# Six 256-column matmuls per weight tile, summed in one PSUM bank per group, in place of two of 512 columns and two of 256 over two banks

## What is computed

```python
def hybrid_layer(x, mem, ...):
    h = rmsnorm(x, g_mix)
    proj = h @ w_in
    fq, fk, fv, ff, lx, lg, mq, gate_logits = jnp.split(proj, cuts, axis=-1)
    ...
    y_fox = forgetting_attention(q, k, v, log_f)
    xr = causal_depthwise_conv(lx, w_lru_conv, b_lru_conv)
    y_lru = rg_lru(xr, w_rg_a, b_rg_a, w_rg_x, b_rg_x, lru_lambda) * jax.nn.gelu(lg)
    mk, mv = jnp.split(rmsnorm(mem, g_mem) @ w_mem_kv, 2, axis=-1)
    ...
    y_mem = memory_attention(qm, km, vm)
    branches = jnp.stack([y_fox, y_lru, y_mem], axis=2)
    y_d = jnp.einsum('bsnc,ncd->bsnd', branches, w_branch)
    gates = jax.nn.sigmoid(gate_logits.reshape(b, s, N_BRANCH, D_MODEL) + b_gate)
    merged = jnp.sum(gates * y_d, axis=2)
    x = x + merged @ w_out
    up = causal_depthwise_conv(rmsnorm(x, g_ffn) @ w_ffn_up, w_ffn_conv, b_ffn_conv)
    u_act, u_val = jnp.split(up, 2, axis=-1)
    return x + (jax.nn.gelu(u_act) * u_val) @ w_ffn_down
```

## Time and profile before

| | us |
|---|---|
| median of 3 runs | 1662.53 |
| lowest and highest run | 1662.39, 1663.37 |
| span of the profiled execution | 1661.6 |
| TensorE matmuls busy in the span | 1641.6 |
| TensorE weight loads busy | 1426.6 |
| VectorE busy | 1117.1 |
| ScalarE busy | 895.9 |

### The profile page before, as it was taken

The page is one execution under the profiler, slowest core; times in us unless marked ns, Lnnn a source line. Parts: engine busy times, 40 slices in busy tenths (PEclk is TensorE's granted clock), DMA queues, the critical chain, the costliest instruction groups (busy, mean ns, idle before and its releaser), DMA issues.

```text
span 1661.6 us, 27207 instructions
## 1 busy us (share of the span) xinstructions
PE 1641.6 (99%) x9356; PEld 1426.6 (86%) x9356; DVE 1117.1 (67%) x1324; ACT 895.9 (54%) x1145; POOL 54.9 (3%) x57
## 2 busy tenths in 40 slices
PE   7999999999999999999999999999999999999998
PEld 6888888888888888888888888888888888888887
DVE  6977677678847566575666777777777777544443
ACT  6766567466644544545455555555555555434332
POOL 0010112000000000000001000000000000000000
PEclk9999999999999999999999999999999999999999
DMA  8544456553555555555565555555555655655653
GB/s 301 195 151 162 150 172 200 188 167 126 177 185 185 191 187 190 189 189 190 177 192 189 176 190 200 189 179 189 192 178 185 202 189 186 201 197 196 202 195 102
DMA packets 85833, 307.37 MB, mean 185 GB/s; under 512 B 9944, under 2 KB 11232, under 8 KB 85664
## 3 DMA queue, kind: packets, MB, share of 16 engines
q1 hardware_dynamic: 84672, 302.89, 55.0%
q0 software_dynamic: 1120, 3.94, 0.8%
HBM read 304.69 MB, written 2.11 MB: 185 GB/s over the span
## 4 chain that ended last, share of the span: by engine, by line
PE 94%; DVE 2%; issue 2%; ACT 1%; DMA 1%; SPq 0%; POOL 0%; ACTq 0%; DVEq 0%; POOLq 0%
PE psG L315 91%; PE psM L315 2%; DVE fox_rstd L910 1%; DVE W L885 1%; DMA mem_raw<-memT 0%; ACT W L554 0%; DMA lru_rg<-w_rg 0%; PE psM L406 0%; ACT fox_rstd L593 0%; DVE fox_S L938 0%; DVE stat L941 0%; DVE fox_q_n L926 0%; ACT L554 0%; ACT fox_S L583 0%; ACT fox_S L605 0%
## 5 line engine op out<-in xcount | busy, mean ns | idle before, releaser
L315 PE MATMUL psG<-X,W 128*128 128x512 f32 (+1 forms) x5632 | 993.2, 338 | 0.0
L315 PEld LDWEIGHTS psG<-X,W 128*128 128x128 f32 x5632 | 860.4, 188 | 128.1 <-issue 2.4
L885 DVE TENSOR_TENSOR W<-raw,W 128x1024 fp32r<-128x1024 f32 x567 | 687.8, 1227 | 314.9 <-ACT W L554 312.2
L554 ACT ACTIVATE W<-raw 128x1024 fp32r<-128x1024 f32 x567 | 591.2, 1054 | 318.7 <-PE psG L315 314.6
L315 PE MATMUL psG<-hidden,W 128*128 128x512 f32 (+1 forms) x1408 | 245.4, 337 | 0.0
L315 PEld LDWEIGHTS psG<-hidden,W 128*128 128x128 f32 x1408 | 214.0, 188 | 31.3
L562 ACT ACTIVATE low<-psG 128x512 f32<-128x512 f32 x140 | 83.8, 598 | 224.6 <-PE psG L315 224.6
L315 PE MATMUL psG<-Y,W 128*128 x768 | 134.4, 337 | 0.0
L315 PEld LDWEIGHTS psG<-Y,W 128*128 128x128 f32 x768 | 117.0, 188 | 17.1
L1300 DVE SCALAR_TENSOR_TENSOR up_c<-up_pad,par_sb,up_c 128x256 f32<-128x256 f32 x176 | 77.5, 482 | 42.3 <-ACT up_c L829 36.3
L315 PE MATMUL psG<-merged,W 128*128 128x512 f32 (+1 forms) x512 | 89.3, 337 | 0.0
(11 more groups left out here) (185 smaller groups left out, 672.5 us busy)
## 6 DMA issues: line engine op xcount, KB each, us to landing
raw<-w_units SPq DMA_DIRECT2D x567, 512.0 KB, 3.4
xs<-xT SPq DMA_DIRECT2D x4, 512.0 KB, 9.8
outT<-xs POOLq DMA_DIRECT2D x7, 256.0 KB, 3.6
mem_raw<-memT SPq DMA_DIRECT2D x3, 512.0 KB, 9.0
lru_rg<-w_rg POOLq DMA_DIRECT2D x8, 128.0 KB, 4.3
c_all<-c_rows POOLq DMA_DIRECT2D x1, 1024.0 KB, 8.8
mem_raw<-memT SPq DMA_DIRECT2D x4, 128.0 KB, 2.5
raw<-w_units SPq DMA_DIRECT2D x2, 256.0 KB, 3.2
```

The lines of the kernel that those rows point to most:

```text
L315: return nc.tensor.matmul(*a, skip_group_check=True, **kw)
L554: nc.scalar.activation(W[:, s, :, 0], raw[:, s], ACT.Copy).then_inc(hi_done, 1)
L885: V.tensor_tensor(W[:, s, :, 1], raw[:, s], f32(W[:, s, :, 0]), ALU.subtract).then_inc(lo_done, 1)
```

## The change

Each weight tile is now worked on by six matmuls of 256 columns. They are ordered by stationary part: for the high weights, half `t` = 0 against high activations, then again `t` = 0 against low activations, then both for `t` = 1; then the low weights against the high activations for both halves (in the `rows_major` phases with weights and activations exchanged). All three products of a half go to the same 256 columns, and both halves lie in one bank, so a group has one bank, `psG` has two, and the sum is complete in PSUM. `start` is set on the first matmul of the bank alone.

So nothing is left to add: `low`, `copy_low`, `add_low` and `yd` are gone, and the reader takes the bank directly. Which engine empties which group is in a table (`EMPTIED_BY`): ACT copies the groups of mv, lru, v, qk and the query of mkq (`empty`) and takes `Tanh` of the gates from the bank; DVE scales the key of mkq, multiplies the branches, adds the residual in out and down, and scales up from the bank. In place of `evac_done` there are two counters, `emptied_act` and `emptied_dve`. Where ACT now writes a destination that a DVE step of the iteration before still reads, ACT waits for that step (`normed` in qk and mkq, `gelu` and `lru_taps` in lru).

```diff
+EMPTIED_BY = {"mv": "aa", "mkq": "da", "lru": "aa", "v": "aa", "qk": "aa", "gate": "aa", "branch": "dd",
+              "out": "dd", "up": "dd", "down": "dddd"}
...
-        psG = ctx.enter_context(nc.psum_tensor("psG", [P, 4, 512], F32))
+        psG = ctx.enter_context(nc.psum_tensor("psG", [P, 2, 512], F32))
...
+        def bank(w):
+
+            return psG[:, w % 2]
+
+        def bank_tiles(w):
+
+            return bank(w).rearrange("p (a t) -> p a t", a=2)
...
-                b = 2 * (w % 2)
-                g = G0[phase] + w
-                if i is not None or g >= 2:
-                    pe.wait_ge(evac_done, at(g - 1, i, NG[phase]) + before[1])
+                if free_act is not None:
+                    pe.wait_ge(emptied_act, free_act)
+                if free_dve is not None:
+                    pe.wait_ge(emptied_dve, free_dve)
...
-                        halves = [slice(t * P, t * P + P) for t in range(2)]
-                        for t, ts in enumerate(halves):
-                            if rows_major:
-                                mm(psG[:, b + t, :], x_hl[:, 0, ts], W[:, s, k], start=kt == 0, stop=False)
-                            else:
-                                mm(psG[:, b + t, :], W[:, s, k, 0, ts], x_hl, start=kt == 0, stop=False)
-                        for t, ts in enumerate(halves):
-                            if rows_major:
-                                ins = mm(psG[:, b + t, T:], x_hl[:, 1, ts], W[:, s, k, 0], start=False, stop=kt == last)
-                            else:
-                                ins = mm(psG[:, b + t, T:], W[:, s, k, 1, ts], x_hl[:, 0], start=False, stop=kt == last)
+                        products = ((0, 0), (0, 1), (1, 0))
+                        for stationary in range(2):
+                            for t in range(2):
+                                ts = slice(t * P, t * P + P)
+                                dst = bank_tiles(w)[:, t]
+                                for w_part, x_part in products:
+                                    if (x_part if rows_major else w_part) != stationary:
+                                        continue
+                                    begin = kt == 0 and w_part == 0 and x_part == 0 and t == 0
+                                    end = kt == last and stationary == 1
+                                    if rows_major:
+                                        ins = mm(dst, x_hl[:, x_part, ts], W[:, s, k, w_part], start=begin, stop=end)
+                                    else:
+                                        ins = mm(dst, W[:, s, k, w_part, ts], x_hl[:, x_part], start=begin, stop=end)
...
-            def copy_low(g, last, i=None, coef=8, groups=2):
+            def empty(last, dst, w, i=None, coef=8):
 
                 act.wait_ge(pe_units, at(last + 1, i, coef))
-                if g >= 2:
-                    act.wait_ge(evac_done, at(g - 1, i, groups))
-                b = 2 * (g % 2)
-                nc.scalar.activation(low[:, g % 2], psG[:, b:b + 2, T:], ACT.Copy).then_inc(low_copied, 1)
+                nc.scalar.activation(dst, bank_tiles(w), ACT.Copy).then_inc(emptied_act, 1)
...
-                    if k in (7, 11):
-                        copy_low(G0[phase] + k // 11, U0[phase] + k - 4, i)
+                    if k == 7 and kind == "lru":
+                        act.wait_ge(lru_taps, i * 3)
+                    if k == 11 and kind == "lru":
+                        wait(dve=side_count("lru", i - 1, "dve", "gelu"))
+                    if k == 7 and kind == "fox" or k == 11 and kind == "mem":
+                        wait(dve=side_count(kind, i - 1, "dve", "normed"))
+                    if k == 11 or k == 7 and kind != "mem":
+                        empty(U0[phase] + k - 4, destination(phase, 0, k // 11), k // 11, i)
                     split(U0[phase] + k, i)
...
-            def add_low(g, dst, i=None, groups=2):
-
-                dve.wait_ge(low_copied, at(g + 1, i, groups))
-                b = 2 * (g % 2)
-                V.tensor_tensor(dst, psG[:, b:b + 2, 0:T], low[:, g % 2], ALU.add).then_inc(evac_done, 1)
...
                     if (k - 4) % per == per - 1:
-                        g = G0["down"] + w
-                        dve.wait_ge(out_done, i * 4 + w) if w else None
-                        add_low(g, yd[:], i, groups=4)
-                        dve.wait_ge(evac_done, at(g + 1, i, 4))
+                        filled(U0["down"] + k - 4, i, 4 * per)
                         tiles = xs[:, bass.ds(i * 8 + 2 * w, 2)]
-                        V.tensor_tensor(tiles, yd[:], tiles, ALU.add).then_inc(out_done, 1)
+                        V.tensor_tensor(tiles, bank_tiles(w), tiles, ALU.add).then_inc(emptied_dve, 1)
```

More of the change, by code:

```diff
@@ L508, in _ @@
             with pe.Fori(0, 4) as i:
-                plain("out", i, {}, operand=lambda kt: merged[:, kt], ready=lambda n: pe.wait_ge(merged_lo, 2 * n + 2))
+                for w in range(2):
+                    group("out", i, w, lambda kt: merged[:, kt], {}, ready=lambda n: pe.wait_ge(merged_lo, 2 * n + 2),
+                          free_dve=emptied("out", i - 1, w))
             def x2_sums():
@@ L782, in quarter @@
                         kind, i, w, n = group
[L783 removed]
+                        if kind == "gate":
+                            act.wait_ge(pe_units, at(QUARTER0 + k - 3, q, QUARTER_UNITS))
+                            if not first and i == 0:
+                                act.wait_ge(acc_added, q * 4)
+                            for t in range(2):
+                                ins = nc.scalar.activation(gates[:, i, w, t], bank_tiles(w)[:, t], ACT.Tanh, scale=0.5,
+                                                           bias=half_bg[:, bass.ds(q * 4 + (i * KT + 2 * w + t), 1)])
+                            ins.then_inc(emptied_act, 1)
                     split(QUARTER0 + k, q, coef=QUARTER_UNITS)
```

206 lines of the change are left out of this document (102 added, 104 removed).

## The result

The changed kernel takes **1714.83 us** (median of 4 runs, 1712.63 to 1714.90) against 1662.83 us for the kernel before on the same chip: 1.0307 times the time, with a 95% interval of 1.0292 to 1.0321. It is 52 us slower. The forecast was 1648 us, faster, with a range up to 1674: wrong in sign and outside its range.

The account below looks back on a forecast made before the run. The prediction took TensorE's matmul pace, 696.7 ns per tile, as the bound. Terms -11.8 - 1.6 - 1.4 = -14.8 us on a span of 1661.6 gave 1646.8, plus 0.9 for the median: 1647.7, rounded to 1648 us; range 1643 to 1674.

Parts of the forecast that it names:

- The bound: From 452 us to the end only TensorE's matmul pace counts: 174.2 ns per matmul, 696.7 ns per tile.
- (a): Matmuls of every weight tile: six of 256 columns take 691.5 ns, 5.2 less than before; -11.8 us over 2272 tiles.
- the pair of 256 behind two 512s: The old tile's two 256-column matmuls, read at 114.7 and 115.8 ns, mean 115.25, taken as the new price.
- The upper bound: Matmuls of every tile: fixed cost from float32 rows, +5.0 ns per tile, +11.4 us; as rival 1670.9 us, chance 0.26.
- The worry about the loads: Six matmuls in a row: loads of 128 columns can follow each other at 108 ns, 7 less than the matmul's 115.
- The fourth rival: Every tile: loads or issue bind in the long row, 119 ns instead of 115, +39 us, 1699 us; chance 0.08.
- the pair and the transposes: Evidence against binding loads or issue: the existing pair of 256 shows 114.7 ns with a load inside, the transposes 107.
- Same columns, one bank, same stationary tile: Matmuls within a tile: adding to the same columns and staying in one bank cost nothing visible; repeated loads win nothing if hidden.
- (b): Emptying of banks by ACT and DVE, from 452 us to the end: hidden behind the matmuls, worth 0.
- (c): Stalls in "qk", TensorE waiting for softmax weights: an add leaves the path, three stalls shorter by 0.6, -1.6 us.
- (d): Tail behind the last matmul: one DVE operation of 0.69 us remains, the last add starts earlier, -1.4 us.

Follow-up runs that it names:

- e1_cut: Kernel before with each 512-column matmul cut in two of 256, old banks, order and emptying kept: 1716.31 us, ratio 1.0319.
- e7_half_cut: Kernel before with only the second 512-column matmul of a tile cut in two of 256: 1697.32 us, ratio 1.0206.
- e14_all_six: Changed kernel, all six matmuls lightened: 192 moving columns in "out", 64 stationary in "up", 224 moving in "down": 1664.27 us, one run.
- e2_turns: Changed kernel with the products in turns, so no stationary tile stands twice in a row and halves alternate: 1714.82 us, ratio 1.0310.
- e10_widths: Changed kernel with four of six matmuls narrower: 248 moving columns in "out", 240 in "up", 224 in "down": 1674.55 us, one run.
- e8_order: Kernel before with a tile's four matmuls ordered 512, 256, 512, 256 columns instead of 512, 512, 256, 256: 1672.27 us, ratio 1.0048.
- e13_kick: e8_order with one small float32 matmul of 128 columns put between every two iterations of "up": 1686.55 us, one run.
- e4_stationary: Changed kernel with fewer stationary columns in four of six matmuls: 96 in "out", 64 in "up", 32 in "down": 1692.28 us, one run.
- e3_moving: Changed kernel with fewer moving columns in four of six matmuls: 224 in "out", 192 in "up", 128 in "down": 1775.27 us, one run.

## Why the prediction was wrong

- **The bound** was right: nothing but TensorE's pace from 452 us to the end, save for the stop at 1578 us, so an error in the pace is an error in the time.
- **(a), the matmuls: the step that failed.** The forecast was -11.8 us, the runs gave +52.9. The sum took 115.25 ns from the pair of 256 behind two 512s and carried it to six in a row, on the ground that each of the two "already has a whole weight load behind or ahead of it". e1_cut shows that a row of 256s by itself costs 120.0 each, and e7_half_cut that the place counts: 117 behind a 512, 120 further on. The upper bound, +11.4 us, came from float32 matmuls and was a fixed cost of 2.5 ns each; it was not a bound at all for a stream in which something else binds.
- **The worry about the loads** was the right one and was weighed wrongly. The 108 ns for a load of 128 columns, read from the earlier trace rows, was a pace of 111.7 in e14_all_six, so the spare time was 3.6 ns of the 115.25 and not 7. And the comparison of the load with the matmul, each by itself, does not give their sum: 111.7 and 113.3 make 120.0. So the sum took each matmul at the larger of two prices, and put what they cost together at nothing. The fourth rival, 119 ns and 1699 us, had the price nearly right with a chance of 0.08; it lacked one ns per matmul (13.6 us) and the break, less the gain of the first units. Its cause, that loads or issue bind by themselves, was half of it: by themselves they allow 111.7. What spoke for it stood in the text ("a row of over six has not been seen at this size"), and against it stood the pair and the transposes.
- **Same columns, one bank, same stationary tile: nothing.** Right, by e1_cut and e2_turns. Loads number 13,900, none is dropped, as was said.
- **(b), emptying: 0** between 452 us and the end. Right; no wait for an emptied bank appears, and DVE and ACT have lost 136 us of work for nothing (166 were forecast).
- **(c), "qk": -1.6 us.** Measured -2.6, which is two things. e1_cut has the old emptying and the slow pace. Its waits for `fox_S` fell to 0.3 us from the 1.7 of the earlier trace rows, and the same stretch of its trace is 2.0 us shorter than the pace alone gives: with a slower TensorE the softmax is simply less late. That leaves 0.6 us for the shorter path itself, where 1.6 was forecast. ACT's wait for `normed` cost nothing, as argued.
- **(d), the tail: -1.4 us.** Right, 0.71 us instead of 2.15.
- **The loop of "down", +4.5 us**, was in no part of the prediction, nor was the gain of 1.7 us in the first units. It counted instructions per matmul for their issue, and not those of a loop's body.

## What to carry to other kernels

A matmul's price in a mixed pattern is the price of its place. Before cutting matmuls, find or make a row in which as many small ones follow each other as will in the new kernel, and take it from there. Where loads are busy for 86% of the span and the change adds half as many again, they are the first suspect. Two prices that are measured one at a time, the load's and the columns', don't give the price of both together: 111.7 and 113.3 made 120.0. Shortening the work of engines that are already hidden pays nothing. Count the instructions of a loop's body too.

## What the runs showed of the hardware

- In a float32r stream with 128 stationary columns, matmuls of 224 or 192 moving columns follow each other in 111.7 ns (e14_all_six). 256 moving columns take 113.3 ns when the loads have 64 columns, and with loads of 128 columns 120.0. Eight moving columns fewer in four of six matmuls (e10_widths) save 26.7 ns per tile.
- A 256-column matmul takes 114.6 to 115.8 ns behind two of 512 (before), 117.2 behind one and about 120 from the second on (e7_half_cut).
- The same code can run at two steady paces, 693.3 and 706.7 ns per tile, 2% apart, for hundreds of microseconds (e8_order, e13_kick). e4_stationary has 706.7 in the first pass of "down" and 700.0 in the second.
- A jump back in a loop of 2112 PE instructions took 4.6 us (after), in one of 1760 also 4.6 us (e7_half_cut), in one of 1408 it took 0.2 us at most (before).
- In e3_moving, with four of six matmuls at 128 moving columns, the granted clock was 1.00 through the first pass of "down". Behind the stop of 4.15 us it was 0.50, the 1.2 GHz level, to the end of the phase, while TensorE was busy for 60 of 60 us. In the kernel after, behind the stop of 2.8 us, it was 0.66 on average from 1581 to 1586 us and then 1.00; in e7_half_cut, behind 2.4 us, it did not fall.
